# Expert weights in transfers of two ring slots: one kernel change on one Trainium2 core

## The reference

```python
def swiglu(x, wg, wu, wd):
    return (jax.nn.silu(x @ wg) * (x @ wu)) @ wd

for e in range(N_EXPERTS):        # 8 experts, D_FF_EXPERT = 1408
    y = y + comb[:, e:e + 1].astype(t.dtype) * swiglu(t, wg[e], wu[e], wd[e])
```

## Time and profile before

| | us |
|---|---|
| median of 3 runs | 1911.96 |
| range of the runs | 1910.83 to 1913.84 |
| time of the profiled execution | 1910.22 |
| its span, first to last instruction | 1908.5 |
| PE busy in it | 1897.8 (99%) |
| DVE busy | 1440.1 (75%) |
| ACT busy | 1165.3 (61%) |
| one expert, from transpose to transpose of block 5 | 94.1 |

### The profile page before, as it was taken

How to read it: one execution, slowest core, us unless ns; L and a number is a source line. 1 busy time by engine, 2 the same in 40 slices (tenths; PEclk the granted TensorE clock), 3 DMA queues, 4 the chain that set the end, 5 groups by cost and what they waited for, 6 DMA issues and landing times.

```text
span 1908.5 us, 25748 instructions
## 1 busy us (share of the span) xinstructions
PE 1897.8 (99%) x8912; PEld 1580.5 (83%) x8912; DVE 1440.1 (75%) x1862; ACT 1165.3 (61%) x1490; POOL 137.2 (7%) x152
## 2 busy tenths in 40 slices
PE   9999999999999999999999999999999999999998
PEld 7888888888888888888888888888888888888887
DVE  8886677547764676566569678898988989888896
ACT  7656644434443444334545667888787878787885
POOL 8300000000000000000200010000000100010101
PEclk9999999999999999999999999999999999999999
DMA  9655566666666666665565468999999999999997
GB/s 358 195 159 164 177 193 193 191 196 192 194 191 195 192 195 190 196 193 187 185 186 167 145 217 337 374 397 385 396 386 398 379 398 378 403 378 403 375 396 258
DMA packets 141572, 510.13 MB, mean 267 GB/s; under 512 B 15937, under 2 KB 15953, under 8 KB 140081
## 3 DMA queue, kind: packets, MB, share of 16 engines
q1 hardware_dynamic: 134288, 486.64, 72.0%
q0 software_dynamic: 7200, 22.39, 4.6%
HBM read 495.33 MB, written 13.64 MB: 267 GB/s over the span
## 4 chain that ended last, share of the span: by engine, by line
PE 98%; DMA 1%; issue 0%; DVE 0%; ACT 0%; POOLq 0%; SPq 0%; DVEq 0%
PE main L637 31%; PE main L639 31%; PE main L638 31%; PE transpose L974 1%; PE transpose L655 1%; PE transpose L1014 0%; DMA raw_pieces<-in_ffn_moe 0%; PE transpose L957 0%; PE transpose L677 0%; DMA raw_pieces<-in_w_in 0%; PE transpose L732 0%; PE transpose L733 0%; PE transpose L731 0%; PE transpose L744 0%; PE spread L712 0%
## 5 line engine op out<-in xcount | busy, mean ns | idle before, releaser
L1423 DVE TENSOR_TENSOR w_low<-raw_pieces,w_high 128x1024 fp32r<-128x1024 f32 x919 | 1099.4, 1223 | 310.9 <-ACT w_high L1075 301.8
L1075 ACT ACTIVATE w_high<-raw_pieces 128x1024 fp32r<-128x1024 f32 x919 | 952.3, 1059 | 293.6 <-DMA raw_pieces<-in_ffn_dense 167.9
L637 PE MATMUL main<-w_high,xT_high 128*128 128x512 f32 (+1 forms) x1856 | 717.5, 387 | 0.3 <-DVE w_low L1544 0.2
L639 PE MATMUL main<-w_high,xT_low 128*128 128x512 f32 (+1 forms) x1856 | 709.7, 382 | 0.0
L638 PE MATMUL main<-w_low,xT_high 128*128 128x512 f32 (+1 forms) x1856 | 708.9, 382 | 0.0
L639 PEld LDWEIGHTS main<-w_high,xT_low 128*128 128x128 f32 x1856 | 348.8, 188 | 68.5
L637 PEld LDWEIGHTS main<-w_high,xT_high 128*128 128x128 f32 x1856 | 349.1, 188 | 66.3 <-issue 1.4
L638 PEld LDWEIGHTS main<-w_low,xT_high 128*128 128x128 f32 x1856 | 349.3, 188 | 65.3
L637 PE MATMUL main<-w_high,hT_high 128*128 128x512 f32 x832 | 329.9, 396 | 0.7 <-DVE hT_low L1839 0.6
L639 PE MATMUL main<-w_high,hT_low 128*128 128x512 f32 x832 | 324.6, 390 | 0.0
L638 PE MATMUL main<-w_low,hT_high 128*128 128x512 f32 x832 | 324.1, 390 | 0.0
(11 more groups left out here) (234 smaller groups left out, 820.3 us busy)
## 6 DMA issues: line engine op xcount, KB each, us to landing
raw_pieces<-in_ffn_moe SPq DMA_DIRECT2D x528, 512.0 KB, 6.3
raw_pieces<-in_ffn_dense SPq DMA_DIRECT2D x264, 512.0 KB, 3.5
raw_pieces<-in_w_in SPq DMA_DIRECT2D x96, 512.0 KB, 3.5
raw_pieces<-in_w_out SPq DMA_DIRECT2D x32, 512.0 KB, 3.6
x_resid<-in_x SPq DMA_DIRECT2D x4, 512.0 KB, 14.8
out_x<-x_resid POOLq DMA_DIRECT2D x4, 512.0 KB, 4.4
xn_rows<-token_major POOLq DMA_DIRECT2D x2, 1024.0 KB, 6.2
token_major<-in_x_t SPq DMA_DIRECT2D x1, 1024.0 KB, 9.7
```

The lines of the kernel that those rows point to most:

```text
L637: pe.matmul(out_ap, lh[ls], rh[rs], start=first, stop=False)
L639: return pe.matmul(out_ap, ll[ls], rh[rs], start=False, stop=last)
L1075: act.activation(WH[:, piece % RING, :], RAWS[:, piece % RING, :], ACT.Copy).then_inc(high_done, 1)
L1423: dve.tensor_tensor(WL[:, piece % RING, :], RAWS[:, piece % RING, :], WH[:, piece % RING, :], ALU.subtract).then_inc(low_done, 1)
```

## The change

The host lays the expert weights out so that for each turn of the ring (11 pieces) the first ten form five pairs, in which each of the 128 rows holds 4 KB of the first piece followed by 4 KB of the second, and the eleventh stands alone. SP loads a pair with one transfer into two neighbouring slots, 8 KB a row, once both slots are free. The pair raises the semaphore of its first slot alone, and ACT waits on that one for both pieces. Nothing of the other engines' work changes, nor do the mixers or the dense part.

```diff
+        def landing(piece):
+            n = piece - PASS[0]["piece"]
+            return raw_full[piece % RING - (1 if n >= 0 and n % RING % 2 else 0)]
...
             def stream_slices(w, n, piece0):
                 with sp.Fori(0, n) as e:
                     for i in range(SLICE_PIECES):
-                        load(w[bass.ds(e, 1), i].rearrange("o p n -> (o p) n"), piece0 + i, e)
+                        turn, at = divmod(i, RING)
+                        if at % 2:
+                            continue
+                        count = min(2, RING - at)
+                        piece = piece0 + i
+                        slot = piece % RING
+                        src = w[bass.ds(e, 1), turn, at * P * PW:(at + count) * P * PW].rearrange("o (p n) -> (o p) n", p=P)
+                        sp.wait_ge(used, e * SLICE_PIECES + (piece + count - RING))
+                        sp.dma_start(RAWS[:, slot:slot + count, :].rearrange("p s n -> p (s n)"), src).then_inc(landing(piece), 16)
...
             def high(piece, shift=0):
-                act.wait_ge(raw_full[piece % RING], shift * (16 * SLICE_PIECES // RING) + 16 * (piece // RING + 1))
+                act.wait_ge(landing(piece), shift * (16 * SLICE_PIECES // RING) + 16 * (piece // RING + 1))
...
-        "ffn_moe": slice_pieces(a["w_gate_moe"][0], a["w_up_moe"][0], a["w_down_moe"][0]),
+        "ffn_moe": in_pairs(slice_pieces(a["w_gate_moe"][0], a["w_up_moe"][0], a["w_down_moe"][0])),
```

More of the change, by code:

```diff
@@ L1910, in slice_pieces, with in_pairs @@
     return np.ascontiguousarray(np.concatenate([a, b, c], 1))
+def in_pairs(pieces):
+    s = pieces.shape[0]
+    turns = pieces.reshape(s, SLICE_PIECES // RING, RING, P, PW)
+    two = turns[:, :, :RING - 1].reshape(s, SLICE_PIECES // RING, RING // 2, 2, P, PW).transpose(0, 1, 2, 4, 3, 5)
+    return np.concatenate([two.reshape(s, SLICE_PIECES // RING, -1), turns[:, :, RING - 1].reshape(s, SLICE_PIECES // RING, -1)], 2)
 def dense_pieces(gate, up, down):
```

## The result

The changed kernel takes 1944.81 us (median of 4 runs, 1942.15 to 1946.06), the kernel before 1911.39 us (median of 4, 1910.55 to 1913.84). The ratio is 1.0171, with a 95% interval from 1.0159 to 1.0183: slower by 33 us. The prediction was 1917.0 us and at most 1922.0. The direction was right, the size wrong by more than six times.

What follows compares the result with a forecast made beforehand. PE was taken as the bound, with DMA also full in the experts. Waits of 1.3 us in the first expert, 6 x 0.45 in the middle and 1.0 in the last gave 5.0 us: 1917.0 us, range 1913.2 to 1922.0.

Steps and rivals of the forecast that it cites:

- Places where the same delay costs nothing: Pieces PE multiplies directly (3.7 us of room), block 5's product and earlier blocks' copies in the experts: no added loss.
- the 1.15 of a full queue: Third expert, DMA queue never empty: pair (52, 53) lands at 1404.96, so PE gets `hT_low` 1.15 us later.
- The prediction's own test: Profile after: PE waiting for `w_low` or `h_blocks`, instead of `hT_low`, would mean the tight place was chosen wrongly.
- The copies of 50 and 51 ... don't stand in the way: Steps 38 and 39: these copies come 2.8 us before, and ACT needs 2.04 us for two, so no delay.
- Issue of the first piece of a pair: SP's load waits for one slot more, so the first piece goes out 1.36 us later; the second as before.
- Which of the two: Idle or full DMA queue: idle chosen from the second expert on, 0.45 us lost in each middle expert.
- Rival B: DMA queue stays full: each middle expert loses 1.15 us, 9.2 us in all, 1921.2 us; chance 0.17.
- Rival C: 1 MB takes 6.2 us to land, as a store did: 14.3 us lost, 1926 us; chance 0.07.
- The sum of separate delays: PE's waits for `hT_low` over the experts, added up: 1.3 + 6 x 0.45 + 1.0 = 5.0 us.
- SP's fewer transfers give nothing: SP issues 36 transfers for 66; SP is on nobody's path, so this is worth nothing.
- rival A: Not slower: big rows load faster, pair (52, 53) landing sooner; 1913.5 to 1915.0 us, nearly all within 0.2%; chance 0.27.
- the 4.0 us from landing to PE: Steps 38 and 39: from the landing of pair (52, 53) through ACT, DVE and `hT_low` to PE, 4.0 us.

Runs made afterwards that it cites:

- Issuing by twos: Kernel before, 512 KB transfers and old layout kept; SP waits for both slots, then issues two single loads: 1919.27 us, ratio 1.0037.
- taking by twos: Kernel before, pieces still loaded singly; ACT takes the first of a pair only when the second has landed too: 1921.91 us, ratio 1.0049.

## Why the prediction was wrong

**"Places where the same delay costs nothing": wrong, and the largest miss.** I checked the pieces that PE multiplies, the product of block 5, and the copies of the earlier blocks ("used ten and more pieces later"). I did not check the products of blocks 0 to 4. They are transposed by PE within a few steps and had 1.1 to 3.9 us of room in experts 2 to 8. With five pairs, PE waits 15.0 us for the products of blocks 0 and 3, for which the sum had nothing. The product of block 5, which I had put at no more than 0.2 us inside the 1.15 of a full queue, adds 2.6. Together they are 17.6 of the 28.0 us of waits. The earlier trace rows even showed PE at such a transpose, but I read from them only when piece 35 was used, not when the product beside it had been ready. The prediction's own test says it: "If PE waits at another line, for `w_low` or `h_blocks`, my choice of the tight place was wrong."

**"The copies of 50 and 51 ... don't stand in the way": wrong.** I gave ACT's 2.04 us as the reason and left out DVE. In the rows of the third expert that I used, DVE's work from 1404.00 on has no pause before `hT_low`. A line shortly before them, which I did not read, is piece 50, the last that DVE waited for, and by only 0.16 us:

```profile
1402.52 1.23 DVE L1423 TENSOR_TENSOR w_low<-raw_pieces,w_high 128x1024 fp32r<-128x1024 f32 x1 [0.16 <-ACT w_high L1075]
```

The single pair at (50, 51) shows that this chain begins at piece 50, and that a delay of its start reaches PE in full. DVE at 84.41 of 94.10 us looked like spare time, but behind a late load it is only the rate at which a delay shrinks, and 0.2 us a piece is slow.

**"Issue of the first piece of a pair", 1.36 us later: unpriced.** I charged only the common landing. Issuing by twos alone costs 7.2 us.

**"Which of the two": wrong.** I took an idle queue from the second expert on, because lost time drains it. The DMA engines did get idle time (share 0.98 to 1.00 over an expert, for 1.02), but a pair landed in 7.1 us, not 4.8 or 5.5. The value 4.8 is right for a half idle queue (4.9 measured). Rival B's full queue, 9.2 us in all, is the size of taking by twos alone (9.9), but that is in part luck: it had everything at `hT_low`, and the trace has 5.1 us of waits there and 3.4 at products. Rival C (6.2 us of landing, 14.3 us in all) was nearer in landing time than either and still held only the `hT_low` part, which measured 10.4, or 11.7 with the 0.16 us of each wait. Its price rests on a misreading. I called 6.2 us the slowest 1 MB transfer of the page, but the page of the kernel before also has a load of 1 MB on SP's own queue, issued among the first pieces of the program:

```profile
token_major<-in_x_t SPq DMA_DIRECT2D x1, 1024.0 KB, 9.7
```

So a 1 MB load behind other loads was on record, at twice my 4.8.

**The sum of separate delays: wrong in kind.** The parts do not add: 7 and 10 make 26. While there is room a delay costs nothing, and once the two together exceed it the rest is paid. A waiting PE also frees slots later, so the next loads are asked for later; how much of the loss that loop makes was not tried by itself. Last, the sum has no term for the clock, which took 1.6 us behind the longest wait.

**Right:** that SP's fewer transfers give nothing (ratio 0.9996 in the dense part); that the row length hardly matters (nothing that can be told at `LEAD` 6, some 2 us at 4, not clear of noise), so that rival A did not come about; the 4.0 us from landing to PE (3.8 measured); and that `hT_low` is waited for in every expert.

**Open.** Why 1 MB in one transfer costs some 6 us more than two of 512 KB that are issued together and taken together. And why, where nothing but weights is moved, a single piece takes 5.4 us to land and not the 3.5 of the dense part, although the rate drops at times: in the kernel before without scatters it is 409 GB/s from 1446 to 1452 us and 348 at a share of 0.97 from 1452 to 1458. So the loss is traced to late pieces on DVE's in-order list, and the lateness to the pairing, but the landing time itself is not explained.

## What to carry to other kernels

Where engines work through one list in order, the room of a load is not that of its own consumer but of the tightest small operation within several pieces behind it. List each of those with its time from "ready" to "used", follow the slower of the preparing engines, and compare the shortest room with the delay of the change before pricing anything. A larger transfer from a ring costs twice, once because its first half is asked for later and once because it may be touched only when the second half is there; two delays that cost 7 and 10 us alone cost 26 together here. If such transfers are wanted, make the room first: here two steps less of `LEAD` took the cost of the pairs from 33 us to some 2, and the same number helped the kernel before by 3 us. And look for long waits of PE: behind four of them, of 1.9 to 2.8 us, the granted clock was 0.50 to 0.51 for some 3 us, so they cost more than their length.

## What was not expected of the hardware

A transfer of 1 MB in rows of 8 KB lands 4.9 us after its issue beside half idle DMA engines, where 512 KB takes 3.6, and 6.6 to 7.5 us in the experts (medians of the kernels here). The Trainium skill's rule of 1 MiB and more in each transfer ("DMA: Bandwidth & Descriptors", rules for kernel authors) brought no bandwidth to this stream, which moved 390 GB/s an expert in 512 KB transfers and 366 to 382 in pairs. It is no fair test of the rule, since PE sets the pace here: with `LEAD` 4 and hardly a wait the pairs move 387 to 391 GB/s. The DMA rate varies from stretch to stretch without other traffic that the trace shows, from 409 to 348 GB/s in neighbouring 6 us without pairs and scatters, and from 400 to 314 within 1451 to 1469 us with pairs and no scatters.
